# Score tiles of 32 columns in the mixer, and an attention loop rebuilt by pairs of heads

## The chip, the cores and the metric

The kernel runs on one core of a Trainium2 chip. The metric is the device time of one execution in microseconds. The engines of the core are named as in the profile: PE is TensorE's matmul, PEld its weight load, DVE is VectorE, ACT is ScalarE, POOL is GpSimd, SP is SyncE.

## What is computed

Two transformer blocks in fp32 over 1024 tokens of width 1024. The change touches two places.

The first block's mixer is an HGRN2 recurrence with six heads of 128 channels. In chunks of tokens it needs the causal scores

```python
diff = jnp.where(causal, b[:, :, :, None, :] - b[:, :, None, :, :], -jnp.inf)
scores = jnp.einsum('bhtk,bhsk,bhtsk->bhts', qb, kb, jnp.exp(diff))
```

The second block has a neighbourhood attention with eight heads of 64 channels on a grid of 16 rows by 64 columns, beside a depthwise convolution of 31 taps over 512 channels:

```python
sc = jnp.einsum("bnqhd,bknjhd->bhnqkj", q_r, k_r).astype(jnp.float32) * scale
sc = jnp.where(mask, sc + bias[None], NEG)
p = jax.nn.softmax(sc.reshape(...), axis=-1)
o = jnp.einsum("bhnqkj,bknjhd->bnqhd", p, v_r)
...
u = _dwconv_centred(u, conv_dw_w[l], conv_dw_b[l])
u = jax.nn.silu(_layernorm(u, conv_ln_g[l], conv_ln_b[l]))
```

## The kernel before

Every activation lies with features on the 128 partitions and the 1024 tokens along them. A projection of 128 output features is one `product` (L681): 8 blocks of input features, each with three fp32r matmuls (high by high, high by low, low by high part) for two halves of 512 tokens, so 48 matmuls. The weights are loaded by SP (`w_raw`), split into high and low parts by POOL (`w_hi`, `w_lo`) and counted in one numbered stream of tiles; `tile_done` tells POOL and SP that a tile has been used.

Order between engines is written out by hand: each engine has its own program, and semaphores (`wait_ge`, `then_inc`) join them. An engine runs its program in order, so a wait holds up all that stands behind it on that engine.

**The head loop** (`head`, five passes of a loop and a sixth written out). The scores of a chunk of 128 tokens are made in a tree: the 128x128 score tile of the diagonal, and seven levels. At level l, blocks of 2^l tokens pair up; ACT writes the decayed keys and queries of the level into `e_t`, TensorE multiplies them (L804), and DVE copies the part that belongs to the level into `s_t` under a mask (`copy_predicated`, L1830). For each of 8 chunks TensorE takes all 128 tokens of the chunk as weights (64 at level 6) and streams the 64 right-hand tokens. The diagonal (L818) takes 128 columns of weights and streams 128. These matmuls are in fp32, which TensorE runs as two instructions ("passes"), so that a count in the profile is twice that in the code. Between the levels stand parts of the projections of this head and the next (`meanwhile`), so that ACT and DVE have time.

**The pair loop** (four passes; `with pe.Fori(0, PAIRS) as p`, and the like on ACT and DVE). A pass does two heads of attention and the convolution of 128 channels. TensorE makes the projections q, k and v, the scores of each unit, the turns and the weighting of v, and the projection of the next pass's convolution input u (`T_PAIRS + 4`). A unit is one head and one of 8 groups of 128 queries, against one to three groups of keys: 16 units a pass. For a unit:

- TensorE: three matmuls of q by k with 64 rows (L1002) into bank 4 or 5
- DVE: adds the bias and takes the row's maximum (L2094), negates it (L2100)
- ACT: exponential and row sum (L1514)
- DVE: reciprocal (L2106), multiplication of the 128x384 probabilities by it (L2108)
- TensorE: turns the probabilities (L720) into bank 6 or 7; ACT copies them into `prob_t` (L1522)
- TensorE: weights v (L1019), with both heads' 128 columns of `v_keys` as weights, into bank 0 or 1, of which 64 rows are used; after four units ACT copies these into `att_t` and adds v's bias (L1541)

DVE does all this between the taps of the convolution (`convolve`, L2042): 15 ahead of the units, 8 behind them, and 8 further taps are made by ACT (`tap_products`, L1489) and summed by POOL (L633). The pass of DVE begins with u_t (L2048, L2051); q is read at L2060, k at L2078, v at L2113. The parts k_lo and q_lo of the fp32r split are DVE's as well; TensorE's first scores wait for both. Most of the next u's product stands behind the last scores:

```python
NEXT_AFTER = {3: [0], UNITS: [1, 2], UNITS + 1: [3, 4], UNITS + 2: [5, 6], UNITS + 3: [7]}
```

Of the kernel before, what the change touches and what calls it, by code (L numbers as in the profile page):

```python
# [22 lines left out]
F32 = mybir.dt.float32  # L23
# [5 lines left out]
P = 128  # L29
# [15 lines left out]
LEVELS = 7  # L45
MASK_W = LEVELS * CHUNK // 2 + CHUNK
# [4 lines left out]
DH = 64  # L51
# [18 lines left out]
TAIL_TAPS = 8  # L70
# [31 lines left out]
NEXT_AFTER = {3: [0], UNITS: [1, 2], UNITS + 1: [3, 4], UNITS + 2: [5, 6], UNITS + 3: [7]}  # L102
# [43 lines left out]
def two_blocks(nc, dram, out):  # L146
    ctx = ExitStack()
    with ctx:
# [3 lines left out]
        def at(name, shape, address, dtype=F32):  # L152
# [14 lines left out]
        eps1, eps2, row_max, neg_max, row_sum, row_inv = (  # L167
            at(name, [P, n], A_CONST + 4096 + 32 * j) for j, (name, n) in enumerate(
                (("eps1", 1), ("eps2", 1), ("row_max", 2), ("neg_max", 2),
                 ("row_sum", 2), ("row_inv", 2))))  # L170
# [10 lines left out]
        def arena(*shapes):  # L181
# [67 lines left out]
            ("v_keys", [P, GROUPS, P], F32), ("bias_raw", [P, 2, 3, P], F32), ("prob_t", [P, 2, WIN], F32),  # L249
            ("bias", [P, 2, 5, P], F32), ("near_mask", [P, 3, P], F32), ("prob", [P, 3, WIN], F32),  # L250
            ("u_t", [P, U_PAD], F32), ("qk32", [P, SEQ], F32), ("conv_pool", [P, SEQ], F32))

        tap_product = sig_cb[:, 0, :]
# [58 lines left out]
        mask_loaded = sem("mask_loaded")  # L312
        bias_stored = sem("bias_stored")
# [97 lines left out]
        neg_max_ready = sem("neg_max_ready")  # L411
        prob_exp = sem("prob_exp")
        inv_ready = sem("inv_ready")
        prob_ready = sem("prob_ready")
        prob_turned = sem("prob_turned")
        prob_t_ready = sem("prob_t_ready")
        prob_t_used = sem("prob_t_used")
# [249 lines left out]
        def _(pe):  # L667
# [126 lines left out]
            def head(h, meanwhile):  # L794

                def level(l, bank):


                    pe.wait_ge(level_ready, h * LEVELS + (l + 1))

                    keys = CHUNK if l < LEVELS - 1 else CHUNK // 2
                    for c in range(NC):
                        e = e_t[:, l % 2, c * CHUNK:(c + 1) * CHUNK]
                        last = pe.matmul(psum[0:keys, bank, c * (CHUNK // 2):(c + 1) * (CHUNK // 2)], e[:, 0:keys],  # L804
                                         level_parts(e, l)[:, :, 1, :], start=True, stop=True)
                    last.then_inc(level_done, 1)
# [188 lines left out]
            def scores(p, s):  # L995

                g, head_rows = s // 2, slice(DH * (s % 2), DH * (s % 2 + 1))
                first, n = key_groups(g)

                pe.wait_ge(scores_max, p * UNITS + (s + 1))  # L1000
                for j, (q, k) in enumerate(((q_hi, k_hi), (q_hi, k_lo), (q_lo, k_hi))):
                    last = pe.matmul(psum[:, 4 + s % 2, 0:n * P], q[head_rows, g * P:(g + 1) * P],  # L1002
                                     k[head_rows, first * P:(first + n) * P], start=(j == 0), stop=(j == 2))
                last.then_inc(scores_done, 1)

            def turn_probabilities(p, s):
                pe.wait_ge(prob_ready, p * UNITS + (s + 1))

                pe.wait_ge(prob_t_ready, p * UNITS + (s + 1))
                _, n = key_groups(s // 2)  # L1010
                turn(prob, 6 + s % 2, [prob[:, s % 3, c * P:(c + 1) * P] for c in range(n)], prob_turned)

            def weigh_values(p, s):
                first, n = key_groups(s // 2)
# [11 lines left out]
            with pe.Fori(0, PAIRS) as p:  # L1026
# [13 lines left out]
                for s in range(2):  # L1040
                    scores(p, s)
# [1288 lines left out]
```

## Time and profile before

| what | value |
|---|---|
| median of 3 runs | 2748.89 us (2746.91 to 2749.15) |
| the profiled execution | 2747.53 us |
| its span, first to last instruction | 2745.6 us |
| PE busy in the span | 2660.2 us |
| DVE, ACT, POOL busy | 1458.2, 643.2, 913.8 us |
| one pass of the head loop | 65.88 us, six heads |
| one pass of the pair loop | 85.7 us, four pairs |

The difference of 1.9 us between the profiled execution and its span lies before the first and behind the last instruction. In the chain view a row is a start, a length and what ran; only pieces that held up the end are listed. In the timeline view a row is a run of like instructions, its length that from the first's start to the last's end. The end of a matmul is modelled, and its duration contains latency, so the spacing of starts says what one costs.

### The profile page before, as it was taken

What the parts mean: (1) busy time and instruction counts of PE and PEld (TensorE: products, weight loads), DVE (VectorE), ACT (ScalarE), POOL (GpSimd) and SP (SyncE); (2) the same over time, 40 slices, a digit from 0 to 9 for tenths busy, and PEclk for the clock granted to TensorE, in tenths of its full rate; (3) what the DMA queues carried; (4) which work ended last, traced back from release to release, by engine and by line L of the source; (5) the groups of instructions that cost most, each with busy time, mean ns of one, the idle gap of its engine ahead of it and who ended that gap; (6) DMA issues with size and microseconds to landing.
All of it is one profiled execution on the core that took longest, in us unless ns stands there. A gap on an engine that the chain in (4) does not pass through costs nothing.

```text
span 2745.6 us, 33855 instructions
## 1 busy us (share of the span) xinstructions
PE 2660.2 (97%) x12569; PEld 2195.7 (80%) x12569; DVE 1458.2 (53%) x1657; ACT 643.2 (23%) x844; POOL 913.8 (33%) x481
## 2 busy tenths in 40 slices
PE   8999999999999999999889889999999999999997
PEld 7888887888888888887667767888878888888886
DVE  7545446343433434357888886224255555555556
ACT  4233334220001010023434444001131111111113
POOL 2222222333333333333434333333333333333333
PEclk9999999999999999999999999999999999999999
DMA  5111112112112111113110001113111111111111
GB/s 201 33 37 31 31 31 85 46 50 57 53 49 60 49 46 53 46 46 116 31 37 29 21 23 46 47 46 115 46 46 47 46 53 46 46 49 51 46 46 77
DMA packets 201585, 144.96 MB, mean 53 GB/s; under 512 B 14095, under 2 KB 183738, under 8 KB 200506
## 3 DMA queue, kind: packets, MB, share of 16 engines
q1 hardware_dynamic: 189604, 122.92, 14.5%
q10 hardware_dynamic: 11926, 21.28, 2.2%
q8 instruction: 37, 0.61, 0.1%
q14 instruction: 18, 0.15, 0.0%
HBM read 131.59 MB, written 14.36 MB: 53 GB/s over the span
## 4 chain that ended last, share of the span: by engine, by line
PE 80%; DVE 14%; issue 4%; ACT 1%; DVEq 1%; DMA 0%; SPq 0%; ACTq 0%
PE psum L681 52%; PE psum L700 16%; DVE conv_t L2042 4%; PE psum L1085 3%; PE psum L804 2%; PE psum L720 2%; DVE h_lo L1685 1%; PE psum L1002 1%; DVE ffn_gate L2218 1%; DVE x_t L1939 1%; PE psum L1185 1%; PE psum L1019 1%; DVE prob L2108 1%; DVE sq_sum L1680 1%; DVE u_t L2051 0%
## 5 line engine op out<-in xcount | busy, mean ns | idle before, releaser
L620 POOL CAST w_hi<-w_raw 128x1024 fp32r<-128x1024 f32 x212 | 239.6, 1130 | 1615.7 <-issue 785.9
L681 PE MATMUL psum<-h_hi,w_hi 128*128 128x512 f32 x2384 | 754.4, 395 | 9.7 <-DVE h_lo L1788 5.4
L681 PE MATMUL psum<-h_lo,w_hi 128*128 128x512 f32 x2384 | 742.7, 391 | 0.0
L681 PE MATMUL psum<-h_hi,w_lo 128*128 128x512 f32 x2384 | 741.4, 390 | 0.0
L622 POOL TENSOR_TENSOR w_lo<-w_raw,w_hi 128x1024 fp32r<-128x1024 f32 x212 | 569.4, 2686 | 17.0
L681 PEld LDWEIGHTS psum<-h_hi,w_hi 128*128 128x128 f32 x2384 | 444.3, 189 | 107.4 <-issue 15.3
L681 PEld LDWEIGHTS psum<-h_lo,w_hi 128*128 128x128 f32 x2384 | 449.4, 188 | 94.5
L681 PEld LDWEIGHTS psum<-h_hi,w_lo 128*128 128x128 f32 x2384 | 449.2, 188 | 94.6
L1939 DVE TENSOR_TENSOR x_t<-x_t,psum 128x512 f32<-128x512 f32 x416 | 281.8, 685 | 193.2 <-PE psum L700 191.0
L2210 DVE TENSOR_TENSOR ffn_z<-psum,rinv 128x1024 f32<-128x1024 f32 x44 | 53.9, 1224 | 272.8 <-PE psum L681 267.2
L700 PE MATMUL psum<-mlp_hi,w_hi 128*128 128x512 f32 x480 | 186.7, 389 | 0.0
L700 PE MATMUL psum<-mlp_lo,w_hi 128*128 128x512 f32 x480 | 186.7, 389 | 0.0
L700 PE MATMUL psum<-mlp_hi,w_lo 128*128 128x512 f32 x480 | 186.7, 389 | 0.0
L1954 DVE SCALAR_TENSOR_TENSOR mlp_a<-psum,rinv 128x1024 f32<-128x1024 f32 x32 | 39.2, 1225 | 235.5 <-PE psum L681 229.9
L2042 DVE SCALAR_TENSOR_TENSOR conv_t<-u_t,cols,conv_t 128x1024 f32 x88 | 147.8, 1680 | 10.0 <-DVE conv_t L2037 0.6
L700 PE MATMUL psum<-ffn_hi,w_hi 128*128 128x512 f32 x320 | 126.8, 396 | 4.1 <-DVE x_t L1939 3.4
L700 PE MATMUL psum<-ffn_lo,w_hi 128*128 128x512 f32 x320 | 124.7, 390 | 0.0
L700 PE MATMUL psum<-ffn_hi,w_lo 128*128 128x512 f32 x320 | 124.7, 390 | 0.0
L633 POOL TENSOR_TENSOR conv_pool<-conv_pool,sig_cb 128x1024 f32<-128x1024 f32 x28 | 68.0, 2430 | 138.1 <-ACT sig_cb L1489 138.1
L1370 ACT ACTIVATE mlp_a<-mlp_a 128x1024 f32<-128x1024 f32 x32 | 34.0, 1062 | 305.4 <-DVE mlp_a L1954 305.4
L700 PEld LDWEIGHTS psum<-mlp_lo,w_hi 128*128 128x128 f32 x480 | 90.1, 188 | 18.7
L700 PEld LDWEIGHTS psum<-mlp_hi,w_lo 128*128 128x128 f32 x480 | 90.1, 188 | 18.7
(284 smaller groups left out, 3008.2 us busy)
## 6 DMA issues: line engine op xcount, KB each, us to landing
w_raw<-in_w_up SPq DMA_DIRECT2D x152, 256.0 KB, 3.1
w_raw<-in_w_in SPq DMA_DIRECT2D x124, 256.0 KB, 3.2
w_raw<-in_w_down SPq DMA_DIRECT2D x108, 256.0 KB, 2.8
w_raw<-in_w_out SPq DMA_DIRECT2D x32, 256.0 KB, 3.1
x_in<-in_x SPq DMA_DIRECT2D x8, 512.0 KB, 8.6
x_spill<-x_t ACTq DMA_DIRECT2D x1, 4096.0 KB, 12.3
x_spill<-x_t ACTq DMA_DIRECT2D x4, 1024.0 KB, 5.1
x_t<-x_spill ACTq DMA_DIRECT2D x1, 4096.0 KB, 12.3
```

The source lines that it names most:

```text
L620: pool.tensor_copy(hi, w_raw[:, slot, :]).then_inc(weight_hi, 1)
L622: pool.tensor_tensor(lo, w_raw[:, slot, :], hi.bitcast(F32), ALU.subtract).then_inc(weight_split, 1)
L633: pool.tensor_tensor(conv_pool[:, :], conv_pool[:, :], tap_product, ALU.add).then_inc(tap_added, 1)
L681: last = pe.matmul(psum[:, first_bank + t, :], w, a[:, k, t * HALF:(t + 1) * HALF], start=(k == 0 and j == 0), stop=(k == KT - 1 and j == 2))
L700: last = pe.matmul(psum[:, 4 + g % 4, :], w, a[:, k, t * HALF:(t + 1) * HALF], start=(k == 0 and j == 0), stop=(k == 1 and j == 2))
L720: last = pe.transpose(psum[:, dst_bank + c // 4, (c % 4) * P:(c % 4 + 1) * P], block_in, ident[:, :])
L804: last = pe.matmul(psum[0:keys, bank, c * (CHUNK // 2):(c + 1) * (CHUNK // 2)], e[:, 0:keys], level_parts(e, l)[:, :, 1, :], start=True, s ...
L1085: last = pe.matmul(psum[:, bank + t, :], w, a[:, k, t * HALF:(t + 1) * HALF], start=(k == 0 and j == 0), stop=(k == 3 and j == 2))
L1939: dve.tensor_tensor(x_d, x_d, psum[:, 4 + g % 4, :], ALU.add).then_inc(down_added, 1)
L1954: dve.scalar_tensor_tensor(mlp_a[:, j, :], banks(2 * j), 0.0, rinv[:, :], ALU.max, ALU.mult)\
L2042: dve.scalar_tensor_tensor(acc, u_t[:, tap:tap + SEQ], w, acc, ALU.mult, ALU.add)\
L2210: dve.tensor_tensor(ffn_z[:, part, :], banks(2 * part), rinv[:, :], ALU.mult).then_inc(ffn_read, 1)
```

## The change

In the mixer the score tiles get `COLS = 32` columns of weights at least. Levels 0 to 4 take four weight tiles of 32 tokens per chunk and stream only the 16 right-hand tokens of the same 32; level 5 takes two of 64, streaming 32; level 6 two of 32, streaming 64; the diagonal four of 32, streaming 32. Each writes its own 32 (or 64) output partitions.

The attention works on a group with both heads at once. The scores' matmuls of the two heads alternate between the two halves of the rows. Weighting v takes each head's 64 columns of `v_keys` alone and writes 64 output partitions, the two heads alternating, all eight groups into banks 0 and 1. The probabilities are no longer normalised: the 16 row sums of a pair are kept, DVE takes their reciprocals at once, ACT spreads them over 64 channels each (`inv_spread`), TensorE turns them by 8 products with the identity, ACT copies them (`inv_wide`) and DVE multiplies the weighted values with them on their way into `att_t`. v's bias is added later, where att_hi and att_lo are made. q's scale and bias and the mask are negated, so that the reduction takes the minimum of negated scores and ACT uses it as it stands. An eighth of the next u's product follows each group; DVE runs one tap after each group, with 12 taps ahead of the groups instead of 15 and 3 behind them. q's product goes to bank 6.

```diff
-NEXT_AFTER = {3: [0], UNITS: [1, 2], UNITS + 1: [3, 4], UNITS + 2: [5, 6], UNITS + 3: [7]}
+NEXT_AFTER = {k + 1: [k] for k in range(KT)}
...
-                    keys = CHUNK if l < LEVELS - 1 else CHUNK // 2
+                    width = min(COLS, CHUNK // 2) if l == LEVELS - 1 else max(COLS, 2 << l)
                     for c in range(NC):
-                        e = e_t[:, l % 2, c * CHUNK:(c + 1) * CHUNK]
-                        last = pe.matmul(psum[0:keys, bank, c * (CHUNK // 2):(c + 1) * (CHUNK // 2)], e[:, 0:keys],
-                                         level_parts(e, l)[:, :, 1, :], start=True, stop=True)
+                        for first in range(0, CHUNK // 2 if l == LEVELS - 1 else CHUNK, width):
+                            begin, tokens = (0, CHUNK) if l == LEVELS - 1 else (first, width)
+                            at_k = c * CHUNK + first
+                            e = e_t[:, l % 2, c * CHUNK + begin:c * CHUNK + begin + tokens]
+                            dst = psum[first:first + width, bank, (c * CHUNK + begin) // 2:(c * CHUNK + begin + tokens) // 2]
+                            last = pe.matmul(dst, e_t[:, l % 2, at_k:at_k + width], level_parts(e, l)[:, :, 1, :],
+                                             start=True, stop=True)
...
-                    last = pe.matmul(psum[:, 6 + c // 4, (c % 4) * P:(c % 4 + 1) * P],
-                                     k_t[:, c * CHUNK:(c + 1) * CHUNK], q_t[:, c * CHUNK:(c + 1) * CHUNK],
-                                     start=True, stop=True)
+                    for first in range(0, CHUNK, COLS):
+                        keys = slice(c * CHUNK + first, c * CHUNK + first + COLS)
+                        at_c = (c % 4) * P + first
+                        last = pe.matmul(psum[first:first + COLS, 6 + c // 4, at_c:at_c + COLS], k_t[:, keys], q_t[:, keys],
+                                         start=True, stop=True)
...
+                pe.wait_ge(scores_max, p * UNITS + (2 * g + 2))
+                for i, (q, k) in enumerate(((q_hi, k_hi), (q_hi, k_lo), (q_lo, k_hi))):
+                    for j in range(2):
+                        rows = slice(DH * j, DH * (j + 1))
+                        done = pe.matmul(psum[:, 4 + j, 0:n * P], q[rows, queries], k[rows, keys],
+                                         start=(i == 0), stop=(i == 2))
...
+            def weigh_values(p, g):
+                first, n = key_groups(g)
+                pe.wait_ge(prob_t_ready, p * UNITS + (2 * g + 4))
                 for c in range(n):
+                    for j in range(2):
+                        head = slice(DH * j, DH * (j + 1))
+                        pe.matmul(psum[head, g // 4, (g % 4) * P:(g % 4 + 1) * P], v_keys[:, first + c, head],
+                                  prob_t[:, g % 2, j, c * P:(c + 1) * P], start=(c == 0), stop=(c == n - 1))
+
+            def turn_inverses(p):
+
+                pe.wait_ge(inv_spread_ready, p + 1)
+                for g in range(GROUPS):
+                    last = pe.matmul(psum[:, 4 + g // 4, (g % 4) * P:(g % 4 + 1) * P], inv_spread[:, g * P:(g + 1) * P],
+                                     ident[:, :], start=True, stop=True)
+                last.then_inc(inv_turned, 1)
...
+                for g in range(1, GROUPS + 2):
+                    if g < GROUPS:
+                        scores(p, g)
+                    if g <= GROUPS:
+                        turn_probabilities(p, g - 1)
+                    if g == 2:
+                        pe.wait_ge(v_tiles_ready, p + 1)
+                    if g >= 2:
+                        weigh_values(p, g - 2)
+                    if g == GROUPS + 1:
+                        turn_inverses(p)
+
+                    if g in NEXT_AFTER:
+                        product(p * 4 + (T_PAIRS + 4), 0, 2, h_hi, h_lo, NEXT_AFTER[g])
+                    if g == 1:
+
                         pe.wait_ge(v_read, p + 1)
-                        turn(v_t, 0, [v_t[:, g * P:(g + 1) * P] for g in range(GROUPS)], v_tiles_turned)
+                        turn(v_t, 0, [v_t[:, c * P:(c + 1) * P] for c in range(GROUPS)], v_tiles_turned)
...
+                exponents(0)
+                for g in range(1, GROUPS + 1):
+                    if g < GROUPS:
+                        exponents(g)
+                    else:
+
+                        act.wait_ge(row_inv_ready, p + 1)
+                        act.activation(inv_spread[:, :].rearrange("p (u c) -> p u c", c=DH),
+                                       row_inv[:, :].unsqueeze(2).to_broadcast([P, UNITS, DH]), ACT.Copy)\
+                           .then_inc(inv_spread_ready, 1)
+                    take_turned(g - 1)
+                    if g == 1:
 
                         act.wait_ge(v_tiles_turned, p + 1)
                         act.activation(v_keys[:, :, :].rearrange("p g v -> p (g v)"), banks(0), ACT.Copy)\
                            .then_inc(v_tiles_ready, 1)
+                    if 2 <= g < 6:
+                        tap_products([4 + g - 2])
+
+                act.wait_ge(inv_turned, p + 1)
+                act.activation(inv_wide[:, :], banks(4), ACT.Copy).then_inc(inv_wide_ready, 1)
...
+                            in1=bias[:, j, at_b:at_b + step * (n - 1) + 1:step, :], scale=1.0, scalar=-3 * NEG,
+                            op0=ALU.add, op1=ALU.min, accum_out=neg_max[:, row:row + 1]).then_inc(scores_max, 1)
+                    if g == 0:
 
                         dve.wait_ge(tile_done, p * 4 + (T_PAIRS + 4))
                         dve.tensor_tensor(by_group(v_t[:, :]), by_row(banks(0)), by_row(rinv[:, :]), ALU.mult)\
                            .then_inc(v_read, 1)
-
-                convolve(range(DVE_TAPS - TAIL_TAPS, DVE_TAPS))
+                    convolve([DVE_TAPS - TAIL_TAPS + g])
+
+                dve.wait_ge(prob_exp, p * UNITS + UNITS)
+                dve.reciprocal(row_inv[:, :], row_sum[:, :]).then_inc(row_inv_ready, 1)
+                convolve(range(DVE_TAPS - TAIL_TAPS + GROUPS, DVE_TAPS))
...
+                dve.wait_ge(inv_wide_ready, p + 1)
+                dve.tensor_tensor(by_row(att_t[:, bass.ds(p, 1), :].rearrange("p a t -> p (a t)")), by_group(banks(0)),
+                                  by_group(inv_wide[:, :]), ALU.mult).then_inc(att_ready, 1)
```

## Rows read from the trace of the kernel before

**Rows 1.** The page: busy time of TensorE, and the chain's shares by engine

```profile
PE 2660.2 (97%) x12569; PEld 2195.7 (80%) x12569; DVE 1458.2 (53%) x1657; ACT 643.2 (23%) x844; POOL 913.8 (33%) x481
PE 80%; DVE 14%; issue 4%; ACT 1%; DVEq 1%; DMA 0%; SPq 0%; ACTq 0%
```

**Rows 2.** Windows: one pass of the head loop, one of the pair loop

```profile
core 0: us, PE busy (x) PEld busy (x) DVE busy (x) ACT busy (x) POOL busy (x), PEclk, DMA share, GB/s
149.98:215.86 65.88, 65.88 (x385) 56.74 (x385) 33.02 (x45) 22.18 (x27) 13.99 (x8) 1.00 0.11 32
...
1392.10:1477.85 85.75, 74.43 (x382) 59.70 (x381) 74.35 (x113) 35.38 (x70) 33.91 (x16) 0.96 0.10 29
```

**Rows 3.** The chain in a head: start us, us, what

```profile
162.24 1.78 PE psum L818 x16
164.03 3.52 PE psum L804 x32
```

**Rows 4.** Timeline of TensorE around level 6: start us, us, instructions

```profile
196.88 0.61 PE L681 MATMUL psum<-h_hi,w_lo 128*128 128x512 f32 x2
197.43 1.15 PE L804 MATMUL psum<-e_t 128*64 128x64 f32 x16
198.50 1.09 PE L720 MATMUL psum<-ident,kd_t 128*128 128x128 f32 x8
```

**Rows 5.** Timeline of TensorE inside level 6 alone

```profile
197.65 0.92 PE L804 MATMUL psum<-e_t 128*64 128x64 f32 x13
```

**Rows 6.** Timeline of TensorE near the end: two matmuls of one column

```profile
2718.51 0.28 PE L1168 MATMUL psum<-ones,sq_sum 128*128 128x1 f32 x2
```

**Rows 7.** Groups of instructions by form: busy us, mean ns, idle before

```profile
L804 PE MATMUL psum<-e_t 128*64 128x64 f32 x96 | 6.9, 225 | 0.0
...
L1489 ACT ACTIVATE sig_cb<-u_t,cols 128x1024 f32<-128x1024 f32 x28 | 31.9, 1138 | 0.0
...
L1514 ACT ACTIVATE prob<-prob,neg_max 128x384 f32<-128x384 f32 x48 | 29.5, 615 | 27.2 <-DVE neg_max L2100 26.5
...
L1522 ACT ACTIVATE prob_t<-psum 128x384 f32<-128x384 f32 x48 | 22.8, 476 | 0.2
...
L1514 ACT ACTIVATION_READ_ACCUMULATOR prob<-prob,neg_max 128x1 f32 x64 | 12.0, 187 | 0.0
```

**Rows 8.** Waits within one pass of the pair loop

```profile
PE psum L1002 <- DVE k_lo L2082: 7.2, 1, 7.2
DVE prob L2094 <- PE psum L1002: 7.0, 10, 1.2
```

**Rows 9.** Timeline of DVE in the second pair

```profile
1434.22 1.21 DVE L2113 TENSOR_TENSOR v_t<-psum,rinv 128x1024 f32<-128x1024 f32 x1
...
1440.04 0.56 DVE L2094 CUSTOM_DVE_ANT_0 prob<-psum,bias 128x384 f32<-128x384 f32 x1 [1.20 <-PE psum L1002]
1440.52 0.08 DVE L2094 DVE_READ_ACCUMULATOR2_ANT row_max<- 128x1 f32 x1
...
1463.87 11.29 DVE L2042 SCALAR_TENSOR_TENSOR conv_t<-u_t,cols,conv_t 128x1024 f32 x8
```

**Rows 10.** The chain through the second pair

```profile
1392.12 3.14 DVE u_t L2051
...
1399.38 3.21 DVE conv_t L2042
...
1427.60 1.11 PE psum L1002 x6
1428.71 4.24 PE psum L681 x12
...
1452.97 0.72 PE psum L1002 x3
1453.68 0.48 PE psum L720 x3
1454.16 0.67 PE psum L1019 x6
...
1477.85 3.14 DVE u_t L2051
```

**Rows 11.** Windows: the stretch of the first scores and the rest of v

```profile
1427.60:1432.90 5.30, 5.30 (x19) 3.95 (x19) 5.03 (x6) 0.20 (x1) 2.03 (x1) 0.64 0.00 0
```

**Rows 12.** The chain around the last pair

```profile
1563.38 3.14 DVE u_t L2051
...
1639.18 2.75 PE psum L681 x12
...
1645.56 12.33 PE psum L681 x54
```

More of the change, by code:

```diff
@@ L992, in _, with scores @@
             product(T_CB + 3, 1, 6, h_hi, h_lo)
-            def scores(p, s):
-                g, head_rows = s // 2, slice(DH * (s % 2), DH * (s % 2 + 1))
+            def scores(p, g):
                 first, n = key_groups(g)
[L1000 to L1014, printed above, removed]
-                pe.wait_ge(prob_t_ready, p * UNITS + (s + 3))
-                pe.wait_ge(att_ready, p * 4 + (s // 4 + 3))
-                for c in range(n):
-                    last = pe.matmul(psum[:, (s // 4) % 2, (s % 4) * P:(s % 4 + 1) * P], v_keys[:, first + c, :],
-                                     prob_t[:, s % 2, c * P:(c + 1) * P], start=(c == 0), stop=(c == n - 1))
-                last.then_inc(prob_t_used, 1)
+                queries, keys = slice(g * P, (g + 1) * P), slice(first * P, (first + n) * P)
@@ new lines, in scores @@
+                pe.wait_ge(scores_max, p * UNITS + (2 * g + 2))
[4 more added lines that the diff above has]
+                                         start=(i == 0), stop=(i == 2))
+                        if i == 2:
+                            done.then_inc(scores_done, 1)
@@ L1495, in _ @@
                 act.wait_ge(q_read, p + 1)
-                act.activation(qk32[:, :], qk32[:, :], ACT.Identity, scale=DH ** -0.5, bias=q_bias[:, bass.ds(p, 1)])\
+                act.activation(qk32[:, :], qk32[:, :], ACT.Identity, scale=-DH ** -0.5, bias=q_bias[:, bass.ds(p, 1)])\
                    .then_inc(q32_ready, 1)
@@ L1558, in _ @@
             for c in range(PAIRS):
-                act.activation(att_hi[:, c, :], att_t[:, c, :], ACT.Copy).then_inc(branch_hi, 1)
+                act.activation(att_hi[:, c, :], att_t[:, c, :], ACT.Identity, bias=v_bias[:, c:c + 1]).then_inc(branch_hi, 1)
             act.wait_ge(ln_summed, 1)
@@ L2079, in _ @@
                    .then_inc(k_read, 1)
-                convolve(range(11, 13))
+                convolve(range(9, 11))
                 dve.wait_ge(k_hi_ready, p + 1)
                 dve.tensor_tensor(k_lo[:, :], qk32[:, :], k_hi[:, :].bitcast(F32), ALU.subtract).then_inc(k_split, 1)
-                convolve(range(13, DVE_TAPS - TAIL_TAPS))
+                convolve(range(11, DVE_TAPS - TAIL_TAPS))
                 dve.wait_ge(bias_ready, p + 1)
-                for s in range(UNITS + 1):
-                    if s < UNITS:
-                        dve.wait_ge(scores_done, p * UNITS + (s + 1))
+                for g in range(GROUPS):
+                    first, n = key_groups(g)
+                    at_b, step = {0: (2, 2), GROUPS - 1: (0, 2)}.get(g, (1, 1))
+                    for j in range(2):
+                        row = 2 * (g % 2) + j
+                        dve.wait_ge(scores_done, p * UNITS + (2 * g + j + 1))
@@ L2148, in _ @@
                 dve.wait_ge(branch_hi, c + 1)
-                dve.tensor_tensor(att_lo[:, c, :], att_t[:, c, :], att_hi[:, c, :].bitcast(F32), ALU.subtract)\
+                dve.scalar_tensor_tensor(att_lo[:, c, :], att_t[:, c, :], v_bias[:, c:c + 1],
+                                         att_hi[:, c, :].bitcast(F32), ALU.add, ALU.subtract)\
                    .then_inc(branch_split, 1)
```

141 lines of the change are left out of this document (51 added, 90 removed).

## The prediction

> **What bounds the kernel now.** I read the first page first: TensorE is busy 97% of the span and carries 80% of the chain that ended last, DVE 14% [rows 1]. Such a mean says nothing of a stage, so the windows view came next, over one pass of each of the two loops that the change touches. In a pass of the head loop (65.88 us, six heads) TensorE is busy for the whole pass at full clock and DVE for half of it. In a pass of the pair loop (85.75 us, four pairs) TensorE is busy 74.4 and DVE 74.4 [rows 2]: neither is full, each waits for the other. So a microsecond of TensorE in the head loop is a microsecond of the result; in the pair loop the order of the waits has to be followed.
>
> The waits view of a pair shows where. TensorE stands 7.2 us before the first scores until DVE has made k_lo, and DVE waits 7.0 us in ten pieces for scores [rows 8]. The chain view then gives each step's length, and two narrow timelines the price of a tile with fewer than 128 columns.
>
> **Part 1, the score tiles.** Before, a head has 8 diagonal tiles, 48 tiles in levels 0 to 5 and 8 in level 6, each of two fp32 passes. Sixteen diagonal passes take 1.78 us and 32 passes of two levels 3.52 us [rows 3]: 0.110 us a pass, although they stream 128 columns in the first case and 64 in the second, so it is the 128 columns of weights that set it. Level 6 has 64 columns of weights; thirteen passes span 0.92 us, of which the last lasts 0.225 (the mean of its form), so one starts every (0.92 - 0.22) / 12 = 0.058 us [rows 5, 7]. Going from 128 to 64 columns saves 0.052; the same slope gives 0.032 us for 32 columns (0.058 - 0.026). Entering and leaving that narrow form costs 0.1 us each time: the last product before it starts at 197.11 and needs 0.23, level 6 starts at 197.43; its last pass starts at 198.36, the next kind at 198.50 [rows 4].
>
> After, the passes of a head are: levels 0 to 4, 5 x 8 x 4 x 2 = 320, and the diagonal 8 x 4 x 2 = 64, all with 32 columns of weights; level 5, 8 x 2 x 2 = 32 with 64 columns; level 6, 32 passes with 32 columns of weights that stream 64. That is 448 instead of 128. 384 x 0.032 = 12.3; level 5 32 x 0.058 = 1.9; level 6 between 32 and 58 ns a pass, 1.4; seven more entries and exits 0.7; together 16.3 us. Before: 96 x 0.110 + 16 x 0.058 + 1.78 = 13.3. So +3.0 us a head, **+18 us for six**, if tiles load their weights one after the other.
>
> Bounds for the pass that no row shows. Above: it costs no less than the 64-column pass, 0.058; then the head needs 448 x 0.058 + 0.7 = 26.7, +80 us in all. Below: the four column groups load side by side, a quarter of 0.032; then 384 x 0.008 = 3.1, level 5 0.9, level 6 0.8, entries 0.7, so 5.5 us a head, -47 in all. I take 0.032 since it is the continuation of two rows, and since two matmuls with one weight load between them do start 0.03 us apart in one place (two records of 0.17 and 0.25 us end within 0.28) [rows 6], so the queue can deliver such pairs. That place is a single one, right after another kind of work, and no proof of a steady rate.
>
> The Trainium skill, TensorEngine Tiling, section Performance Considerations, speaks against this part: a matmul of one column takes as long as one of 60, so a factor should not be taken out of a dimension that is already small. At the full clock 60 cycles are an estimated 25 ns, which is under the load and would leave the sum as it is; the trace agrees in so far as 64 and 128 streamed columns cost the same 0.110 us.
>
> **Part 2, attention.** The time is counted from the start of u_t L2051 (1392.12), which comes again at 1477.85, 85.73 us later; the first scores start at +35.5 [rows 10].
>
> Ahead of the scores DVE runs two taps fewer before k_lo (11 instead of 13). Eight taps take 11.29 us, so a tap 1.43 [rows 9]: the scores start at +32.6 (call it S). k and q are long done by then on TensorE. The stall is shorter but still there, so I keep the slow clock behind it: the six first matmuls 1.11 us and the last 12 of the v product 4.24 instead of 2.75, with a mean granted clock of 0.64, so mostly at the 1.2 GHz level [rows 10 to 12]. v is done at S+5.35. DVE, whose queue now has the v_t read right behind the two first reductions, waits there 2.7 us (it is late only for itself).
>
> One group (both heads) on TensorE. Scores: before 2 x 0.72 [rows 10]. Alternated over the two row groups they run side by side, as the first six already do at the slow clock (six of 256 columns take 1.11 us in all, latency among it, where six in a row would need six times 0.21 at 1.2 GHz). Then six weight loads of 0.11 set it, 0.67, with the entry 0.85; if not side by side, 1.45. Turns 6 x 0.11 = 0.7. Values: 12 passes, now of 64 columns of weights at 0.058 = 0.7 and the entries 0.2: 0.9, against 2 x 0.67 before [rows 10]; if halves of the columns don't overlap, their 128 fp32 columns keep 0.11 a pass, 1.5. Product of the next u: an eighth of it is 6 matmuls at 2.75 / 12 [rows 12], 1.37, and some 0.1 for the change of form, 1.45. Sum 3.9 us a group, of which the product was behind the loop before. DVE needs in a group two reductions of 0.56 + 0.08 with gaps and a tap: 2.8. ACT needs two exponentials with their sums 2 x 0.80, two copies 2 x 0.48 and a tap product 1.14: 3.7 [rows 7, 9]. So TensorE leads, narrowly.
>
> The course: g=1 (scores, turn, product, turn of v) ends at S+9.1. g=2 waits 0.4 for the reduction that stands behind v_t and a tap, and 1.1 for v_keys, which ACT makes behind two exponentials: S+14.2. g=3 to 7: 5 x 3.9 less 0.2, S+33.5. g=8 without scores 2.8, S+36.3. The last values 0.7 and the inverses, 8 real fp32 products of two passes, 16 x 0.110 = 1.8 (new): S+38.9. ACT's copy of two banks 1.1, DVE's multiplication into att_t 1.3 (new), u read 1.4: S+43. The three last taps and the pool sum (5.7 us) lie before that wait and are done. ACT's spreading of the inverses, 1.1, stands ahead of the last two copies but is ready at scores(7)+5.2, when TensorE comes for them at +5.6: hidden with 0.4 to spare. Period 32.6 + 43 = 75.6.
>
> Taps inside the loop meet GpSimd's tap sums: a tap that takes 1.29 alone took 3.21 when one ran [rows 10]. Four such meetings can lift DVE's group from 2.8 to 4.7 against TensorE's 3.9, up to 3.4 us; I take 1.5, as the meetings are partial. **Period 77.1 instead of 85.7.** Of the normalisation DVE loses 16 x (0.15 + 0.15) and 16 multiplications of 0.42 to 1.6 us, but as DVE waits anyway, this shows only through the period.
>
> Three periods give 3 x 8.6 = 26. In the last pair no u follows; gate_b's product starts at 1645.56, 82.2 us after its mark [rows 12], and would wait for att_t at about S+41.7 = +74.3, with 1.5 for GpSimd 75.8: 6.4. Four att_lo with an added operand and four biased copies of att_hi, +1.3. Negating the mask once 0.3, under the first u. The bias loads keep their place on ACT's queue; SP's loads follow the products as before. Attention: 26 + 6.4 - 1.3 = **-31 us**. If neither kind of tile runs side by side, a group costs 5.1 and the period is about 85: then only some -3.
>
> **Sum.** Profiled execution 2747.53 (span 2745.6), +18 - 31 = 2734.5; the median of the runs is 1.4 above it: **2736 us**.
>
> **Rivals.**
> - A, side by side. Column groups load and multiply at the same time, so a 32-column pass costs 8 to 25 ns. For it: two row groups demonstrably overlap [rows 10]. Against: even there a load follows a load by about 0.1 us. At 8 ns 2749 - 47 - 31 = 2671, at 20 ns (head 11.8 us) 2709; middle 2690. The skill's TensorEngine Tiling, section Key Properties, says that different tiles load and multiply in parallel and that a change of mode drains the array; by it this rival is right, and the 0.1 us of the rows agrees with the drain.
> - B, the other side: a floor per pass. 448 passes instead of 128; if one load and one matmul cost 45 ns to hand over, a head is 384 x 0.045 + 1.9 + 1.4 + 0.7 = 21.3, +8 a head, +48: 2766; at 0.058 2798. It decides from 0.038 us a pass on, where +31 eats the attention's gain. For it: no row has a steady rate under 0.058.
> - C, the clock. Four stretches of thin work a head might lower the granted clock (1.00 now); a fall costs what the v product shows, 1.5 us [rows 10]: 24 x 1.5 = 36, 2772. Against: the whole pass of the head loop, its level stretches among it, ran at 1.00 [rows 2].
> - D, attention gains little, since column halves don't overlap or DVE with GpSimd leads: period 83 or more, 2758.
>
> **Chances.** Forecast 0.38, A 0.27, B 0.20, C 0.05, D 0.10. 0.2% is about what a measurement here tells from no change (5.5 us). Faster: 0.30 of the forecast, all of A, 0.03 of B and D, 0.60. Same: 0.06 + 0.03 + 0.02, 0.11. Slower 0.29. The forecast's own range is 2722 to 2748; the whole one reaches to the middle of A and over most of B and C, 2680 to 2776.
>
> **What would show it.** L804's start-to-start: 0.032 us, about 13.6 us a head for L804 (now 11.5), and a head period near 69. In the pair: L2051 to L2051 near 77, the stall before L1002 some 6 to 7 us, a group's x6 scores in 0.85, L1019's passes at 0.058. The prediction is wrong if the 32-column pass is far from 0.032 either way, which weighs six times 384 passes, or if the group on DVE or ACT grows beyond 3.9.

## The result, and the profile after

| | before | after |
|---|---|---|
| median | 2749.02 us (2746.91 to 2750.23, 4 runs) | 2665.82 us (2665.62 to 2667.09, 4 runs) |
| span of the profiled execution | 2745.6 us | 2663.9 us |

The ratio is 0.9699, 95% interval 0.9682 to 0.9716: 83 us faster. The prediction was 2736 us with a range of 2680 to 2776. The sign was right, the time lies 70 us below the forecast and 14 below the range. It is close to rival A's lower end (2671).

Lines have moved: `product` is L683 (was L681), the levels L810 (L804), the diagonal L827 (L818), the scores L1012 (L1002), the values L1031 (L1019), the turn L722 (L720), u_t L2070 and L2073 (L2048, L2051), the taps L2064 (L2042), the reduction L2113 (L2094).

First the page of the kernel after: TensorE's busy time, and the shares of the chain (compare [rows 1]).

```profile
PE 2597.5 (98%) x14553; PEld 2123.1 (80%) x14553; DVE 1429.8 (54%) x1474; ACT 633.6 (24%) x820; POOL 925.7 (35%) x481
PE 87%; DVE 8%; issue 3%; ACT 2%; DVEq 0%; DMA 0%; SPq 0%; ACTq 0%
```

TensorE issues 1984 instructions more and is busy 63 us less. DVE's share of the chain fell from 14 to 8%. The windows view of one pass of each loop (compare [rows 2]):

```profile
core 0: us, PE busy (x) PEld busy (x) DVE busy (x) ACT busy (x) POOL busy (x), PEclk, DMA share, GB/s
142.99:201.84 58.85, 58.85 (x705) 48.78 (x705) 34.10 (x45) 22.11 (x27) 14.44 (x8) 1.00 0.12 36
1344.21:1416.14 71.93, 67.23 (x398) 52.12 (x397) 66.67 (x67) 33.00 (x64) 37.51 (x15) 0.98 0.12 35
```

A head takes 58.85 us instead of 65.88, a pair 71.93 instead of 85.75. Following the same place through both traces gives the account. The product behind the six heads starts at 437.03 instead of 472.80 us, 35.8 earlier. The first u_t of the pair loop (L2073) keeps that, 1270.19 instead of 1305.90. Three periods then give 38.3 (219.2 against 257.5 us) and the last pair 10.6, so gate_b's product starts at 1560.96 instead of 1645.56, 84.6 earlier. A little further on it is 85.2, which holds until 2590. The last 75 us give 3.5 back, and 81.7 is the difference of the spans. So **the mixer gave 35.8 us, the attention 49.4, and the end lost 3.5**. The forecast had +18, -31 and 0.

Next the timeline of TensorE in a head, the score tiles alone (compare [rows 4]; before, 32 passes of two levels held up the chain for 3.52 us [rows 3]):

```profile
155.19 0.76 PE L827 MATMUL psum<-q_t,k_t 128*32 128x32 f32 x64
155.78 1.31 PE L810 MATMUL psum<-e_t 128*32 128x16 f32 x128
169.06 1.41 PE L810 MATMUL psum<-e_t 128*32 128x16 f32 x128
176.04 1.81 PE L810 MATMUL psum<-e_t 128*32 128x16 f32 x96
183.44 1.09 PE L810 MATMUL psum<-e_t 128*32 128x64 f32 x32
```

and its groups by form:

```profile
L810 PEld LDWEIGHTS psum<-e_t 128*32 128x32 f32 x2112 | 24.5, 110 | 7.8 <-issue 7.5
L810 PE MATMUL psum<-e_t 128*32 128x16 f32 x1920 | 21.0, 185 | 2.2 <-issue 2.2
```

128 passes span 1.41 us, of which the last lasts 0.185: one starts every (1.41 - 0.185) / 127 = 0.0096 us. A single weight load is still recorded with 110 ns, but 1920 matmuls of 185 ns occupy only 21.0 us together: they overlap many times. A duration in such a group is a latency and no price. Level 5 (the last 32 of the x96) comes out at (1.81 - 0.61 - 0.22) / 31 = 0.032 us and level 6 at (1.09 - 0.22) / 31 = 0.028.

The chain through the second pair (compare [rows 10]):

```profile
1370.41 4.07 issue
1374.47 1.01 PE psum L1012 x6
1375.48 4.03 PE psum L683 x12
...
1391.46 0.72 PE psum L1012 x6
1392.19 0.81 PE psum L722 x6
1392.99 0.81 PE psum L1031 x12
1393.80 1.59 PE psum L683 x6
...
1409.84 0.59 PE psum L1031 x8
1410.42 1.98 PE psum L1038 x16
```

The stall before the first scores, the 4.07 us of "issue", is 4.1 us instead of 7.2; DVE's k_lo ends just ahead of the scores, at 1374.37. A group of both heads costs 0.72 + 0.81 + 0.81 + 1.59 = 3.93 us. Scores of both heads take what one head's took before (0.72 for x3). The new products that turn the inverses (L1038) lie bare on the chain with 1.98 us.

The chain at the end, after and then before, with the windows of the two stretches:

```profile
2607.24 9.95 PE psum L702 x30
```

```profile
2692.43 7.09 PE psum L700 x30
```

```profile
2601.90:2621.90 20.00, 16.59 (x63) 13.13 (x62) 12.49 (x14) 1.26 (x2) 7.36 (x4) 0.83 0.09 27
```

```profile
2683.60:2703.60 20.00, 16.57 (x72) 12.74 (x71) 15.34 (x18) 2.29 (x3) 9.34 (x4) 1.00 0.07 26
```

The same thirty matmuls take 2.9 us longer, at a mean granted clock of 0.83 in these 20 us against 1.00. That is most of the 3.5 us lost. In both kernels TensorE had been idle for 3.4 us of the stretch, just ahead of them, so the idle time alone doesn't explain the lower clock.

### The profile page after: what moved, and what is told of

It reads as the page before. It is cut to its first block, busy times and chain, and to the rows that moved or that the text cites. A ratio compares the mean times of both kernels' runs of the same rounds, so it can differ in the third digit from the quotient of the medians.

```text
span 2663.9 us, 37431 instructions
## 1 busy us (share of the span) xinstructions
PE 2597.5 (98%) x14553; PEld 2123.1 (80%) x14553; DVE 1429.8 (54%) x1474; ACT 633.6 (24%) x820; POOL 925.7 (35%) x481
## 4 chain that ended last, share of the span: by engine, by line
PE 87%; DVE 8%; issue 3%; ACT 2%; DVEq 0%; DMA 0%; SPq 0%; ACTq 0%
PE psum L683 59%; PE psum L702 17%; PE psum L1105 3%; DVE h_lo L1704 2%; PE psum L722 1%; DVE ffn_gate L2234 1%; PE psum L810 1%; PE psum L1031 1%; DVE x_t L1958 1%; PE psum L1205 1%; PE psum L1012 1%; DVE sq_sum L1699 1%; DVE ffn_val L2238 0%; DVE ffn_gate L2238 0%; DVE ffn_val L2234 0%
## 5 line engine op out<-in xcount | busy, mean ns | idle before, releaser
L683 PE MATMUL psum<-h_hi,w_hi 128*128 128x512 f32 x2384 | 757.4, 397 | 13.6 <-DVE h_lo L1807 6.8
L683 PE MATMUL psum<-h_lo,w_hi 128*128 128x512 f32 x2384 | 743.4, 391 | 0.0
L683 PE MATMUL psum<-h_hi,w_lo 128*128 128x512 f32 x2384 | 742.9, 391 | 0.0
L624 POOL TENSOR_TENSOR w_lo<-w_raw,w_hi 128x1024 fp32r<-128x1024 f32 x212 | 575.1, 2713 | 17.0
L683 PEld LDWEIGHTS psum<-h_hi,w_hi 128*128 128x128 f32 x2384 | 443.8, 189 | 115.6 <-issue 20.2
L683 PEld LDWEIGHTS psum<-h_hi,w_lo 128*128 128x128 f32 x2384 | 449.6, 189 | 95.1
L683 PEld LDWEIGHTS psum<-h_lo,w_hi 128*128 128x128 f32 x2384 | 449.6, 189 | 95.0
L2064 DVE SCALAR_TENSOR_TENSOR conv_t<-u_t,cols,conv_t 128x1024 f32 x88 | 182.5, 2074 | 5.9 <-DVE conv_t L2059 0.6
L702 PEld LDWEIGHTS psum<-mlp_hi,w_hi 128*128 128x128 f32 x480 | 90.1, 188 | 18.7
## 6 DMA issues: line engine op xcount, KB each, us to landing
x_spill<-x_t ACTq DMA_DIRECT2D x1, 4096.0 KB, 12.3
x_t<-x_spill ACTq DMA_DIRECT2D x1, 4096.0 KB, 12.3
```

Of the source, the lines that this page charges most:

```text
L624: pool.tensor_tensor(lo, w_raw[:, slot, :], hi.bitcast(F32), ALU.subtract).then_inc(weight_split, 1)
L683: last = pe.matmul(psum[:, first_bank + t, :], w, a[:, k, t * HALF:(t + 1) * HALF], start=(k == 0 and j == 0), stop=(k == KT - 1 and j == 2))
L702: last = pe.matmul(psum[:, 4 + g % 4, :], w, a[:, k, t * HALF:(t + 1) * HALF], start=(k == 0 and j == 0), stop=(k == 1 and j == 2))
L2064: dve.scalar_tensor_tensor(acc, u_t[:, tap:tap + SEQ], w, acc, ALU.mult, ALU.add)\
```

## The experiments

Each ran beside the kernel before, whose medians were 2750.5 (experiments 1 to 4), 2749.5 (5 to 8) and 2749.8 (9 and 10). Ratios are to these.

**1. tiles_only**, the kernel before with the new score tiles alone.

```diff
 # the kernel before
+COLS = 32
 ... (the level and diagonal loops of the change, L810 and L827)
```

> The kernel before with part 1 alone (score tiles of 32 columns, attention as it was). Theory: the parts add up. The marks of the two traces put 35.8 us of the gain ahead of the second block, so this run gives 2749 - 36 = 2713 us, head period 58.9 instead of 65.9. Rival: the two parts share the gain through the TensorE queue or the clock, then it is off by more than 4 us from 2713.

Measured: 2718.6 us (2713.1 to 2721.4), ratio 0.9888 (0.9871 to 0.9904), span 2711.3. The head period is 58.9 us, and the product behind the heads starts at 438.39. **The mixer alone gives 34.4 us** by this mark, where the forecast had a loss of 18. The median misses the expected 2713 by 5.6 us, more than the 4 that the expectation allowed. The profiled execution (2713.1) is the fastest of the four and had a mean granted clock of 0.991; the other three had 0.987 to 0.988 and took 2718.6 to 2721.4 us. By medians this part gives 31.9 us.

**2. attention_only**, the changed kernel with the old tiles.

```diff
-COLS = 32
+COLS = 128
```

> The changed kernel with the tiles of the mixer back at 128 columns (64 at level 6), so part 2 alone. Theory of added parts: 2749 - 49.5 = about 2700 us (with up to 3.5 more if the last stage again falls to the lower clock level), pair period 72, head period 65.9. What was forecast for this part was -31, so 2718.

Measured: 2699.76 us (2699.12 to 2701.16), 0.9817 (0.98 to 0.9833), span 2698.0. Some 260 us behind the pair loop it is 51.3 us ahead of before. 34.4 + 51.3 = 85.7, against 85.2 for both at that place. By medians it is 31.9 + 50.8 = 82.7, against 83.2. Either way the two parts add up.

**3. same_group.** The same tiles in another order: all 8 chunks of one column group, then the next group, so that neighbouring matmuls use the same 32 columns of the array.

```diff
-                    for c in range(NC):
-                        for first in range(0, CHUNK // 2 if l == LEVELS - 1 else CHUNK, width):
+                    for first in range(0, CHUNK // 2 if l == LEVELS - 1 else CHUNK, width):
+                        for c in range(NC):
...
-                for c in range(NC):
-                    for first in range(0, CHUNK, COLS):
+                for first in range(0, CHUNK, COLS):
+                    for c in range(NC):
```

> The changed kernel, but the tile loop outside the chunk loop in levels and diagonal: the same instructions, of which eight tiles in a row now go to the same column group before the next group's turn. Theory that successive column groups run side by side: a pass now costs what one group needs alone, about 0.032 us, so a head grows by 384 x (0.032 - 0.009) = 8.8 us, five full heads and part of the sixth, 2666 + 44 to 53 = 2710 to 2719. Rival, a 32-column pass is cheap in itself (9 ns whatever group it goes to): 2666, no change.

Measured: 2707.15 us (2705.78 to 2708.28), 0.9844 (0.9827 to 0.986): 41 us slower than the changed kernel, by order alone, and 3 us under the expected range. The product behind the heads starts at 478.11 instead of 437.03, so the whole loss lies in the mixer. Its timeline of TensorE in the same head:

```profile
180.14 3.52 PE L810 MATMUL psum<-e_t 128*32 128x16 f32 x128
189.28 3.67 PE L810 MATMUL psum<-e_t 128*32 128x16 f32 x96
198.55 1.78 PE L810 MATMUL psum<-e_t 128*32 128x64 f32 x32
```

(3.52 - 0.18) / 127 = 0.026 us a pass instead of 0.0096, level 6 (1.78 - 0.22) / 31 = 0.050 instead of 0.028. The mean still contains some overlap, since the 128 passes change their group seven times. The first thirteen, all in one group, show the bare step in a narrower window:

```profile
180.14 0.58 PE L810 MATMUL psum<-e_t 128*32 128x16 f32 x13
```

(0.58 - 0.18) / 12 = 0.033 us. So one column group alone costs what the forecast said, 0.032. The fall to 0.0096 comes from neighbours that lie in different column groups. In this order the narrow tiles don't pay: a head takes 66.76 us, 0.9 more than with the old tiles (65.88).

**4. cols_64.** `COLS = 64`: two column groups of 64, half as many passes.

```diff
-COLS = 32
+COLS = 64
```

> The changed kernel with COLS = 64: two column groups. Theory side by side: a 64-column pass alone is 0.058, two groups in turn make it 0.029; 192 passes of levels 0 to 5 and 32 of the diagonal 6.5 us, level 6 as before 0.9 (one group only), 7.4 and entries against about 6 now: +1.5 to 2.5 us a head, 2675 to 2680. Rival, cost by columns only: 240 x 0.058 = 13.9 us, +8 a head, 2706 to 2714.

Measured: 2676.85 us (2672.1 to 2677.95), 0.9727 (0.971 to 0.9743). In the timeline:

```profile
174.28 2.06 PE L810 MATMUL psum<-e_t 128*64 128x32 f32 x64
```

(2.06 - 0.22) / 63 = 0.029 us a pass. A 64-column pass with nothing beside it cost 0.058 [rows 5]; two side by side halve it. The time lies in the expected range. Twice as many passes of 32 columns are still better: 2.0 us a head (58.85 against 60.87) and 11 us between the medians, 8 by the ratios.

**5. scores_by_head.** All three score matmuls of one head, then those of the other.

```diff
-                for i, (q, k) in enumerate(((q_hi, k_hi), (q_hi, k_lo), (q_lo, k_hi))):
-                    for j in range(2):
+                for j in range(2):
+                    for i, (q, k) in enumerate(((q_hi, k_hi), (q_hi, k_lo), (q_lo, k_hi))):
```

> The changed kernel, scores of a group written as three matmuls of head 0 and then three of head 1, instead of alternating. In the kernel before, the first six (written in just this order) started 0.11 us apart in pairs, one of each head. Theory, TensorE's queue lets work on another row group pass: no change, 2666 and 0.72 us a group. Rival, the alternation makes the overlap: a group takes 1.1 to 1.4 us, 7 groups x 4 pairs x 0.4 to 0.7 = 11 to 20 us more, 2677 to 2686.

Measured: 2664.88 us (2661.89 to 2667.18), 0.9688 (0.9674 to 0.9703), no difference from the changed kernel. Its timeline pairs the matmuls by their operands:

```profile
1394.95 0.45 PE L1012 MATMUL psum<-k_hi,q_hi 64*128 64x384 f32 x2
1395.23 0.34 PE L1012 MATMUL psum<-k_lo,q_hi 64*128 64x384 f32 x2
1395.41 0.34 PE L1012 MATMUL psum<-k_hi,q_lo 64*128 64x384 f32 x2
1395.68 0.87 PE L722 MATMUL psum<-ident,prob 128*128 128x128 f32 x6
```

0.73 us from the first to the next kind, as with the alternating order. The two heads use different halves of the rows, and the queue runs them beside each other even where three matmuls of the one stand ahead of the other's. So here TensorE did not start its matmuls strictly in the order of the program, as "an engine runs its program in order" would have it.

**6. values_by_head.** The same for the values, whose two heads use different halves of the columns.

```diff
-                for c in range(n):
-                    for j in range(2):
+                for j in range(2):
+                    for c in range(n):
```

> The changed kernel, the weighting of v written head by head (all key groups of head 0, then of head 1), so that successive passes stay on one half of the columns. Theory as for the scores (the queue lets the other column half pass): no change. Rival, only neighbours in program order overlap: 12 passes of 128 fp32 columns at 0.11 us, 1.3 instead of 0.81 us a group, 7.3 x 4 x 0.5 = 15 us more if TensorE leads the loop throughout, 2681.

Measured: 2672.53 us (2669.89 to 2675.37), 0.9717 (0.9702 to 0.9732), 7 us slower than the changed kernel and 8 slower than experiment 5, which ran beside it. The chain:

```profile
1392.46 0.81 PE psum L722 x6
1393.27 1.07 PE psum L1031 x12
```

1.07 us for twelve passes instead of 0.81: between the two theories. Here the order matters, other than for halves of the rows, but it loses 0.26 us a group and not the 0.5 that a full loss of the overlap would cost. Three periods take 225.3 us instead of 219.2.

**7. inverses_turned.** The inverses turned by 8 transposes (`turn`) instead of 8 real products.

```diff
-                for g in range(GROUPS):
-                    last = pe.matmul(psum[:, 4 + g // 4, (g % 4) * P:(g % 4 + 1) * P], inv_spread[:, g * P:(g + 1) * P],
-                                     ident[:, :], start=True, stop=True)
+                turn(inv_spread, 4, [inv_spread[:, g * P:(g + 1) * P] for g in range(GROUPS)], inv_turned)
```

> The changed kernel with the 8 products by the identity (16 passes, 1.98 us a pair) replaced by 8 transposes of one pass (0.9 us). Theory: they stand alone on the path from the last values to att_t and to the next u read, so each pair gains 1.0 us, 4 in all: 2662. Rival, DVE is the bound of a pair by now (its taps stretched by GpSimd): it waits only 1.0 us for the inverses, so up to that is gained and no more; the same number here, but then DVE's wait ahead of att_t vanishes in the trace.

Measured: 2659.92 us (2657.99 to 2663.76), 0.968 (0.9667 to 0.9694). The chain:

```profile
1410.53 0.59 PE psum L1031 x8
1411.12 1.02 PE psum L722 x8
1412.14 5.92 PE psum L683 x26
```

1.02 us instead of 1.98, four times: 3.8. Behind the pair loop it is 4.3 us ahead of the changed kernel. The profiled executions differ by 7.7 us, and the rest of that lies at the end, where the thirty matmuls took 7.10 us instead of 9.95. The medians differ by 5.9 us. The rival's sign is in the trace too: DVE's waits ahead of att_t fall from 4.3 us in four pairs to 0.3. So DVE has nothing left to spare there. **This version is the fastest measured**, by 0.2%. Its times lie under all of the changed kernel's, but the intervals of the two ratios overlap.

**8. pool_taps_6.** Two taps fewer on ACT and POOL, two more on DVE, both behind the groups.

```diff
-POOL_TAPS = 8
+POOL_TAPS = 6
-TAIL_TAPS = 11
+TAIL_TAPS = 13
...
-                    if 2 <= g < 6:
+                    if 2 <= g < 4:
```

> The changed kernel with 6 of the 31 taps on ACT and GpSimd instead of 8, and 25 on DVE instead of 23 (two more behind the groups). Theory, a tap sum of GpSimd (2.4 us) stretches a DVE tap by about as much as a tap costs alone (3.06 to 3.21 against 1.28): within 3 us of 2666. Rival, DVE's own count bounds the pair: 2 x 1.43 x 4 = 11 us more, 2677.

Measured: 2681.34 us (2679.06 to 2681.72), 0.9748 (0.9735 to 0.9762), 15 us slower, a pair 75.9 us. The theory missed, and the rival fell 4 us short. DVE's timeline at the end of a pair:

```profile
1413.57 9.45 DVE L2064 SCALAR_TENSOR_TENSOR conv_t<-u_t,cols,conv_t 128x1024 f32 x5
1423.16 1.23 DVE L2132 TENSOR_TENSOR conv_t<-conv_t,conv_pool 128x1024 f32 x1
```

TensorE's last product of the pair ends at 1419.87. The pool sum, which stands ahead of att_t on DVE's queue, starts only at 1423.16. So DVE is the engine that the next pair waits for. In the changed kernel it is late by nothing there and waits 1.0 us, which is less than one tap.

**9 and 10. pool_taps_9, pool_taps_10.** The other way, on the version of experiment 7: one or two taps more on ACT and POOL. The values for ten taps stand in brackets. The expectation says that the first tap taken from DVE is the last ahead of k_lo. In the code it isn't: 11 taps stand ahead of k_lo as before, and the one that goes is the single tap between k_lo and the first reduction. The second is one behind the groups.

```diff
-POOL_TAPS = 8
+POOL_TAPS = 9          (10)
-TAIL_TAPS = 11
+TAIL_TAPS = 11         (10)
...
-                    if 2 <= g < 6:
+                    if 2 <= g < 7:         (8)
```

> The version with turned inverses, with one convolution tap more made by ScalarE and summed by GpSimd (9 instead of 8, VectorE 22 instead of 23; the tap that goes is the last ahead of k_lo). Theory, VectorE's own count bounds the pair: a tap is 2.07 us in the mean, so the first scores start 2 us earlier, the stall of 4 us ahead of them shrinks to 2, and four pairs give 8 us: about 2652. In the run with 6 taps on GpSimd the reverse cost 15 us for two taps, 1.9 a tap and pair. Rival, TensorE's eight groups bound what stands behind the first scores and GpSimd's longer service slows VectorE's taps or the weight parts by as much: 2660 (2656 to 2664).

> As the run with 9 taps, with 10 taps on ScalarE and GpSimd and 21 on VectorE: 11 ahead of the scores, one in each of 8 groups, 2 behind. Theory, VectorE's count bounds the pair: what a tap behind the scores gives is small, as VectorE has up to 1 us to spare at the end of a pair in that version; so about 2650. Rival, GpSimd: eight taps in a pair of 71 us are 8 x 1.7 us more than half its time with the split weights, and two taps more (ScalarE's products in the groups 6 and 7) hold up the weight parts of the next pair: 2655 to 2670, with TensorE waiting for w_lo at the start of a pair.

Measured: 2676.48 us (2675.86 to 2678.17), 0.9731 (0.9714 to 0.9747), and 2670.44 us (2670.18 to 2674.59), 0.9713 (0.9696 to 0.973), both slower than the version they were built on, by 17 and 11. My theory missed both. The rival's sign was right: for ten taps its range just misses the 2670.4, for nine it expected no more than 2664. POOL's timeline with nine taps, then DVE's:

```profile
1396.83 2.39 POOL L635 TENSOR_TENSOR conv_pool<-conv_pool,sig_cb 128x1024 f32<-128x1024 f32 x1 [1.54 <-ACT sig_cb L1506]
1400.78 2.39 POOL L635 TENSOR_TENSOR conv_pool<-conv_pool,sig_cb 128x1024 f32<-128x1024 f32 x1 [1.55 <-ACT sig_cb L1506]
```

```profile
1397.26 3.06 DVE L2061 SCALAR_TENSOR_TENSOR conv_t<-u_t,cols,conv_t 128x1024 f32 x1
1401.19 3.06 DVE L2061 SCALAR_TENSOR_TENSOR conv_t<-u_t,cols,conv_t 128x1024 f32 x1
```

A DVE tap that starts just behind a POOL sum ends 1.1 us after that sum (1400.32 against 1399.22) and lasts 3.06 us, where one alone lasts 1.28. So a tap given to POOL frees 1.28 us and costs 1.8 on another tap when the two meet. DVE's total for its taps but the first hardly changes with 22, 21 and 20 of them (45.6, 44.7, 44.8 us). The Trainium skill, SBUF — State Buffer, section Who interferes with whom, says that a VectorE instruction with two inputs in SBUF contends with a GpSimd instruction that reads SBUF, and that the ports they share are an exclusive lock. The tap's end at 1.1 us behind the sum, near the 1.28 that it needs alone, agrees within 0.2.

Two things explain the loss. First, nothing was gained ahead of the scores: from u_t to the first scores of the second pair it is 30.2 to 30.3 us with eight, nine and ten taps alike. Where the tap went, DVE now waits for TensorE: with nine 1.3 us for the scores and 3.2 for v's product, instead of 1.3 for the latter alone. Second, the end of a pair grew. DVE with eight taps on POOL (experiment 7), from the tap of the last group to the pool sum, and then with nine:

```profile
1405.71 1.27 DVE L2061 SCALAR_TENSOR_TENSOR conv_t<-u_t,cols,conv_t 128x1024 f32 x1
1407.13 4.14 DVE L2061 SCALAR_TENSOR_TENSOR conv_t<-u_t,cols,conv_t 128x1024 f32 x3
1411.41 1.84 DVE L2129 TENSOR_TENSOR conv_t<-conv_t,conv_pool 128x1024 f32 x1
```

```profile
1408.79 3.32 DVE L2061 SCALAR_TENSOR_TENSOR conv_t<-u_t,cols,conv_t 128x1024 f32 x1
1412.25 4.69 DVE L2061 SCALAR_TENSOR_TENSOR conv_t<-u_t,cols,conv_t 128x1024 f32 x3
1417.08 3.20 DVE L2129 TENSOR_TENSOR conv_t<-conv_t,conv_pool 128x1024 f32 x1
```

The ninth tap's sum meets DVE's tap of the last group (3.32 instead of 1.27 us), and the pool sum now falls on POOL's weight part (3.20 instead of 1.84). From the tap of the last group to the next u_t DVE takes 13.95 us instead of 10.16. So u_t starts 7.1 us behind the start of TensorE's next product instead of 3.7, and the first scores wait 7.4 us in the third pair (7.7 in the second) instead of 4.0. With ten taps DVE has one tap fewer at that end: u_t starts 5.6 us behind the product, and the scores wait 5.9. That is why nine is worse than ten: three periods take 226.9 against 223.3 us (216.0 with eight), and the end at the lower clock, seen with nine and not with ten, accounts for about 3 us more.

The chain with ten taps shows a third engine at its limit inside the groups:

```profile
1398.54 2.40 POOL conv_pool L635
1401.07 1.16 ACT sig_cb L1506
1402.48 2.39 POOL conv_pool L635
```

ACT's next product of a tap waits for POOL's sum of the last one, and the sum for the product, so this ring takes 3.94 us, as long as TensorE's group (3.93). In the changed kernel POOL's sums in the groups start 3.92 to 3.95 us apart too.

## Why the prediction was wrong, step by step

**The step that failed: the 32-column pass at 0.032 us, "if tiles load their weights one after the other".** Rival A's sentence, that column groups load and multiply at the same time, is what the chip does. Worked out again with the measured steps, a head has 384 x 0.0096 = 3.7, level 5 1.0, level 6 0.9 and the entries 0.7, together 6.3 us in place of 16.3; before it was 13.3. That is -7.0 a head, and the period shows -7.03. It holds for five heads. The sixth gained only 0.8: TensorE waits there for DVE and ACT (kd_t, h_hi and h_lo), which a cheaper tile doesn't move. So the mixer gave 35.8, where rival A at its lower bound had 47. **This one step is 54 of the 70 us.** The value itself was right for one column group: experiment 3 shows 0.033 a pass where neighbours share their columns, 0.026 in the mean, and a head 0.9 us longer than before. What I misjudged was that the change's loop order puts four different groups next to each other, which is the very condition of the rival, and a rule of the Trainium skill that I cited for it (TensorEngine Tiling, Key Properties) said so. My argument against was that "even there a load follows a load by about 0.1 us", but those were loads of 128 columns in half of the rows, with no row on loads of different columns.

The rule that I weighed against this part (TensorEngine Tiling, Performance Considerations, that a factor shouldn't be taken out of a dimension that is already small) would have spoken for keeping the tiles. Within one column group it fits: a pass costs 33 ns there (26 in the mean of experiment 3), not less than the estimated 25 ns of its 60 cycles, and the narrow tiles lose 0.9 us a head. Side by side it doesn't: in the changed kernel and in experiment 1 a pass with 16 streamed columns fell to 9.6 ns, and the head gained 7.0 us.

**Attention, the right mechanism with sizes too high: -49.4 instead of -31.** The stall before the scores remains and shrinks, a group costs 3.93 us against 3.9 predicted. That TensorE leads is not clear, as DVE and the ring of ACT and POOL (experiments 9 and 10) take just as long. The terms inside the group were each off and cancelled (scores 0.72 not 0.85, turns 0.81 not 0.7, values 0.81 not 0.9, product 1.59 not 1.45). What was too high:
- The stretch from u_t to the first scores, 30.3 us and not 32.6. I only took two taps off. In the new order u_t (L2073) meets no weight part of POOL's and takes 1.29 instead of 3.14, and q_lo 1.2 instead of 2.05.
- The 1.5 us for meetings of taps with POOL inside the groups did not come: a tap of 3.06 (2.98 to the next start) and two reductions, 0.48 apart, just fit into 3.93.
- The stretch from the first scores to the next u_t is 41.7 and not 43; v, the first groups and v_keys were each some tenths earlier. The steps of the prediction themselves add up to S+42.6, which it rounded to 43.

That makes 71.9 in place of 77.1 for the second pair; the three periods are 74.0, 71.9 and 73.3, together 12.3 us better than the forecast (38.3 instead of 26). The last pair gave 10.6 instead of 6.4. The 1.3 us for biased copies at its end did not show: there the lead grew by 0.6. Together 18.4.

**The end** cost 3.5 us that I had at nothing, 2.9 of them in the thirty matmuls at the lower clock. Rival C had looked for the clock in the mixer, where it stayed at 1.00.

54 + 18 - 3.5 = 69, against 70 between forecast and median.

Right were: 0.1 us to enter a narrow form (the account of the head closes with it), the scores of two row halves side by side, ACT's spreading hidden, the inverses at 1.8 (1.98) on the path, and rival D's fear of column halves, in part (experiment 6). Rivals B and C did not occur.

## What to carry to other kernels

A price per matmul read from a form where neighbours share the same columns of the array is not the price of a mix of column groups: before costing narrow tiles, look at which columns neighbouring matmuls use, and order the loop so that they differ. Where one engine leads by tenths of a microsecond, removing its work pays only until the next engine's count is full; here one tap more on GpSimd cost 17 us, two more 11, and two fewer 15. Moving vector work to GpSimd frees little when the two meet on a tap: count the meetings, not the instructions. And look at what stands right behind the instruction that you remove: where the engine then waits anyway, nothing is gained.

## What the runs showed of the hardware

- Four column groups of 32 side by side: an fp32 pass every 9.6 ns, though each weight load is recorded with 110 ns and each matmul with 185. With eight tiles of one group in a row the same pass costs 33 ns inside the group and 26 in the mean. The Trainium skill, TensorE: Matmul & The Clock Gate, Part 3 (Packing small matmuls), gives about 4 ns for each further tile of a pack and measured gains for row and column packs; the direction agrees.
- Two groups of 64 columns: 29 ns a pass, against 58 for one.
- Halves of the rows run side by side whichever way the program orders them (0.73 against 0.72 us a group); halves of the columns gain most when they alternate (0.81 against 1.07 us).
- A DVE tap behind a GpSimd sum lasts 3.06 us instead of 1.28.
- The granted clock fell near the end in some profiled kernels (0.83 over 20 us in the changed one and in experiments 2 to 6, 8 and 9; 1.00 in the kernel before and in experiments 1, 7 and 10), in the thirty matmuls behind 3.4 us of TensorE standing idle. The same 3.4 us stand in all twelve profiles, so they don't decide it alone. What does was not settled.
